# Two transformer blocks on one core: order of the gated units, their low part and one sum within each feed-forward step

## The reference, cut to what matters

```python
ffn = (jax.nn.silu(h2 @ w_gate[l]) * (h2 @ w_up[l])) @ w_down[l]
x = x + gt2 * ffn
...
h = h + (jax.nn.silu(y @ w_gate[i]) * (y @ w_up[i])) @ w_down[i]
```

## Time and profile before

| what | value |
|---|---|
| median of 3 runs | 2380.46 us (2379.41 to 2380.8) |
| the profiled execution, its own time | 2379.61 us |
| span of the profile (first to last instruction) | 2377.9 us |
| TensorE busy | 2244.1 us, 94% |
| VectorE busy | 1938.7 us, 82% |
| ScalarE busy | 1365.9 us, 57% |
| mean granted clock of TensorE | 0.996 |
| steps with gate, up and down together | 20 (10 in each network) |

### The profile page before, as it was taken

The page is one execution under the profiler, slowest core; times in us unless marked ns, Lnnn a source line. Parts: engine busy times, 40 slices in busy tenths (PEclk is TensorE's granted clock), DMA queues, the critical chain, the costliest instruction groups (busy, mean ns, idle before and its releaser), DMA issues.

```text
span 2377.9 us, 30985 instructions
## 1 busy us (share of the span) xinstructions
PE 2244.1 (94%) x10284; PEld 1760.2 (74%) x10284; DVE 1938.7 (82%) x2192; ACT 1365.9 (57%) x1688; POOL 87.9 (4%) x124
## 2 busy tenths in 40 slices
PE   6999999998999999999999999989999999999998
PEld 3577657876777777777778887867777777777786
DVE  4377788989888889988885998688898888888865
ACT  3233475565666666666665444546666666666654
POOL 1101030000000000000010000000000000000020
PEclk9999999999999999999999999999999999999999
DMA  9999986755655565656646555655555565656554
GB/s 392 415 364 371 383 325 239 305 189 167 195 185 188 185 192 179 189 186 187 195 150 214 177 185 169 230 176 186 189 182 186 186 193 187 193 185 191 180 177 151
DMA packets 131567, 518.23 MB, mean 218 GB/s; under 512 B 14497, under 2 KB 20257, under 8 KB 118305
## 3 DMA queue, kind: packets, MB, share of 16 engines
q1 hardware_dynamic: 121552, 449.11, 57.5%
q0 software_dynamic: 9216, 67.11, 6.9%
q10 hardware_dynamic: 720, 0.99, 0.1%
HBM read 512.96 MB, written 4.19 MB: 217 GB/s over the span
## 4 chain that ended last, share of the span: by engine, by line
PE 48%; DVE 20%; issue 9%; ACT 5%; DVEq 1%; DMA 0%; ACTq 0%; SPq 0%
PE ps L2495 28%; PE ps L2673 17%; DVE sum_w_lo L1686 5%; DVE w_lo L1679 3%; ACT w_hi_more L975 3%; DVE sum_raw L1725 2%; DVE sum_raw L1704 2%; DVE w_lo L1969 2%; DVE raw L1710 1%; DVE raw_more L1710 1%; ACT sum_w_hi L864 1%; PE ps L2483 1%; ACT w_hi L975 1%; PE ps L2637 1%; DVE gate L2238 1%
## 5 line engine op out<-in xcount | busy, mean ns | idle before, releaser
L975 ACT ACTIVATE w_hi<-raw 128x1024 fp32r<-128x1024 f32 (+1 forms) x432 | 447.5, 1048 | 352.3 <-PE ps L2673 258.0
L1969 DVE TENSOR_TENSOR w_lo<-raw,w_hi 128x1024 fp32r<-128x1024 f32 (+1 forms) x242 | 292.6, 1218 | 153.1 <-ACT w_hi L975 148.6
L2673 PE MATMUL ps<-w_hi,fm_hi 128*128 128x512 f32 (+1 forms) x840 | 331.4, 394 | 6.9 <-DVE w_lo L1969 5.2
L2673 PE MATMUL ps<-w_lo,fm_hi 128*128 128x512 f32 (+1 forms) x864 | 334.2, 387 | 0.0
L864 ACT ACTIVATE sum_w_hi<-sum_raw 128x1024 fp32r<-128x1024 f32 x180 | 189.6, 1053 | 204.6 <-DVE sum_raw L1704 149.0
L2673 PE MATMUL ps<-w_hi,fm_lo 128*128 128x512 f32 (+1 forms) x776 | 299.6, 386 | 0.0
L1686 DVE TENSOR_TENSOR sum_w_lo<-sum_raw,sum_w_hi 128x1024 fp32r<-128x1024 f32 x180 | 219.5, 1220 | 50.0 <-ACT sum_w_hi L864 47.7
L1679 DVE TENSOR_TENSOR w_lo<-raw,w_hi_more 128x1024 fp32r<-128x1024 f32 x180 | 214.6, 1220 | 16.8 <-ACT w_hi_more L975 13.0
L1679 DVE TENSOR_TENSOR w_lo<-raw,w_hi 128x1024 fp32r<-128x1024 f32 x180 | 218.0, 1220 | 7.5
L975 ACT ACTIVATE w_hi_more<-raw 128x1024 fp32r<-128x1024 f32 x198 | 201.9, 1048 | 35.8 <-DVE raw L1710 29.7
L2673 PEld LDWEIGHTS ps<-w_hi,fm_hi 128*128 128x128 f32 x840 | 157.7, 188 | 63.1 <-issue 23.7
(11 more groups left out here) (399 smaller groups left out, 4631.7 us busy)
## 6 DMA issues: line engine op xcount, KB each, us to landing
raw<-in_w_up SPq DMA_DIRECT2D x152, 512.0 KB, 3.5
raw<-in_w_down SPq DMA_DIRECT2D x132, 512.0 KB, 3.5
ada_raw<-in_w_ada POOLq DMA_DIRECT2D x64, 1024.0 KB, 10.7
raw<-in_w_in SPq DMA_DIRECT2D x120, 512.0 KB, 4.0
raw<-in_w_gate SPq DMA_DIRECT2D x112, 512.0 KB, 4.0
raw<-in_w_out SPq DMA_DIRECT2D x64, 512.0 KB, 3.6
raw_more<-in_w_gate SPq DMA_DIRECT2D x64, 512.0 KB, 3.5
raw_more<-in_w_down SPq DMA_DIRECT2D x44, 512.0 KB, 3.5
```

The lines of the kernel that those rows point to most:

```text
L975: act.activation(hi_tile(like)[:, :, 0:width], raw_tile(like)[:, :, 0:width], ACT.Copy).then_inc(hi_ready, 1)
L1969: dve.tensor_tensor(lo_tile(p)[:, :, 0:width], raw_tile(p)[:, :, 0:width], hi_tile(p)[:, :, 0:width], ALU.subtract).then_inc(lo_dve, 1)
L2673: last = pe.matmul(banks[t][:, 0:width], a, b, start=kt == 0 and k == 0, stop=kt == kts - 1 and k == 2)
```

## The change

Five edits, all of order:

- TensorE transposes the gated units behind the first form `b11`, ahead of `c`.
- VectorE makes `hid_lo` behind the low parts of b21 and of sum w, no longer ahead of sum z.
- ScalarE rounds sum u of the next step ahead of the last `sums_out` of this step, no longer at the head of the step.
- At the head of a feed-forward VectorE does `early(0)` ahead of `hidden_first`, and the three `mixed_rest` stand between low parts; ScalarE rounds two mixtures ahead of one weight block.
- `ungated` is cleared by one memset on GpSimd, and ScalarE waits for it (`cleared`) ahead of its first `early_his`.

```diff
-TURN_AFTER = ("c", 0)
+TURN_AFTER = ("b11", 0)
...
             def gate_up_his(i):
 
-                sum_hi(i, "u", 0)
                 hidden_hi(i + done + 1)
...
+            splits(f + UP + AHEAD + 1, f + UP + AHEAD + 2)
+            mixture_hi(0)
+            mixture_hi(1)
+            splits(f + UP + AHEAD + 2, f + UP + AHEAD + 3)
+            mixture_hi(2)
             splits(f + UP + AHEAD + 3, a)
+            if not done:
+                act.wait_ge(cleared, 1)
             early_his(0, 0)
             early_his(0, 1)
+            sum_hi(0, "u", 0)
             with act.Fori(0, FFN_STEPS - 2) as i:
                 gate_up_his(i)
                 down_his(i)
                 early_his(i + 1, 0)
                 sums_out(i, 2)
                 early_his(i + 1, 1)
+                sum_hi(i + 1, "u", 0)
                 sums_out(i, 3)
...
             mla_operands()
+            pool.wait_ge(emb_spilled, 16)
+            pool.memset(ungated[:, :, :], 0.0).then_inc(cleared, 1)
             pool_block2(pool, rests, rest_loop)
...
                 sum_low(i, "u", 0)
-                hidden_lo(i + done + 1)
                 sum_z(i, 0)
                 piece_low(i, "b21", 0)
                 sum_low(i, "w", 0)
+                hidden_lo(i + done + 1)
                 piece_low(i, "c", 1)
...
             mix_operands(1)
-            rests(f + UP + 2, f + UP + 3)
+            rests(f + UP + 2, f + UP + 4)
+            mixed_rest(0)
+            rests(f + UP + 4, f + UP + 5)
             mix_operands(2)
-            rests(f + UP + 3, f + UP + 4)
-            for k in range(GROUPS):
-                mixed_rest(k)
-            rests(f + UP + 4, f + UP + 6)
-            if not done:
-                dve.wait_ge(emb_spilled, 16)
-            clear(0)
-            rests(f + UP + 6, a)
-            clear(1)
+            rests(f + UP + 5, f + UP + 6)
+            mixed_rest(1)
+            rests(f + UP + 6, f + UP + 7)
+            mixed_rest(2)
+            rests(f + UP + 7, a)
+            early(0)
             hidden_first()
-            early(0)
```

More of the change, by code:

```diff
@@ L489, in build @@
         y_ready, sub_ready, sub_squared = sem("y_ready"), sem("sub_ready"), sem("sub_squared")
-        pool_step = sem("pool_step")
+        pool_step, cleared = sem("pool_step"), sem("cleared")
         x_ready, x_cols, x_squared = sem("x_ready"), sem("x_cols"), sem("x_squared")
@@ L939, in act_ffn, with mixture_hi @@
             act.sem_inc(gate_read, 1)
-            splits(f + UP + AHEAD + 1, f + UP + AHEAD + 3)
-            for k in range(GROUPS):
+            def mixture_hi(k):
                 act.wait_ge(mixed_raw, GROUPS * (1 if done else 0) + k + 1)
                 act.activation(mixed_hi[k][:, :, :, :], mixed_tiles[k][:, :, :, :], ACT.Copy).then_inc(mixed_hi_ready, 1)
+            splits(f + UP + AHEAD + 1, f + UP + AHEAD + 2)
[3 more added lines that the diff above has]
+            mixture_hi(2)
             splits(f + UP + AHEAD + 3, a)
+            if not done:
+                act.wait_ge(cleared, 1)
             early_his(0, 0)
             early_his(0, 1)
+            sum_hi(0, "u", 0)
             with act.Fori(0, FFN_STEPS - 2) as i:
@@ L1843, in rests @@
                     rest(p)
-            def clear(t):
-                if not done:
-                    link(dve.memset(ungated[:, t, :], 0.0))
             rests(f + UP if done else f + AHEAD + 3, f + UP)
```

## The result

The changed kernel takes **2309.97 us** (median of 4 runs, 2306.3 to 2310.75) beside 2380.63 us for the kernel before; the ratio is 0.970, with a 95% interval of 0.968 to 0.972. The profiled execution took 2310.75 us, its span is 2309.0 us. The forecast was 2308, its range 2298 to 2333.

What follows compares the result with a forecast made beforehand. The prediction took VectorE's late run, which TensorE waits for, as the bound. Steps 18 x 3.13 = 56.3 plus heads 16.2 gave 72.5 off 2379.61, so 2307.1, or 2308 us as a median; range 2298 to 2333.

Steps and rivals of the forecast that it cites:

- Period: One feed-forward step, repeating every 67.16 us before: claimed to take 64.03 us, 3.13 less.
- W: Point in each step where TensorE starts the last form w; forecast at 575.9 in the first network.
- T: Point in each step where TensorE's transposes of the gated units start; forecast at 541.95 in the first network.
- slot of 2.44: Rival: the operation moved into VectorE's run costs 2.44 us, pause included, 1.3 more than the rows' spacing; 2332 us; chance 0.02.
- the rival: ScalarE's 1.2 us of room between the `ungated` copy and `hid_hi` closes, eating the turn's gain; 2357 us; chance 0.06.
- So it does the low part of sum u and sum z at once: VectorE at the step's end, after b22's low part at 680.0: both done by about 682.3, cover 2.6 us.
- Late weight block: Rival: sum z asks for b21 some 7 us earlier and its load is late; periods stay, 2364 us; chance 0.04.
- up to 0.3 more per head: Clock loss in each head: 1.65 us lost again after TensorE's wait makes its path 33.9, adding up to 0.3 us.
- Gain 8.6: Head of the first feed-forward: W at 575.9 instead of 584.5, 8.6 us earlier.
- Gain 8.2: Head of the second feed-forward: W at 1611.1 instead of 1619.3, 8.2 us earlier.
- Sum: Whole run: 18 periods give 56.3 us and heads 16.2, together 72.5 off the profiled 2379.61.
- TensorE becomes the bound: Rival: waits in VectorE's run shrink too, so TensorE's own work sets a period of 62.3; 2277 us; chance 0.03.

Runs made afterwards that it cites:

- lo_back: The changed kernel with VectorE's `hid_lo` put back ahead of sum z in each step; 2316.26 us.
- z_run: The changed kernel with sum z of the second group computed a second time into a spare tile, inside VectorE's run from b21's low part to the last form; 2331.46 us.
- head_back: The changed kernel with both heads as before: old order on VectorE and ScalarE, memsets on VectorE, none on GpSimd; steps stay changed; 2321.71 us.
- turn_back: The changed kernel with the transposes of the gated units put back behind the conventional product `c`; 2363.27 us.
- turn_only: The kernel before with only the transposes of the gated units moved behind the first form `b11`; 2328.9 us.
- z_gap: The changed kernel with sum z of the first group computed a second time into a spare tile, where VectorE stands idle ahead of b21's low part; 2307.32 us.
- b21_lo_place: The changed kernel with ScalarE rounding the first group's b21 a step earlier, `hid_lo` directly behind b21's low part, and an own tile for the second group's sum u; 2273.01 us.
- sum_back: The changed kernel with ScalarE's rounding of the first group's sum u put back at the head of each step; 2312.43 us.
- b21_early: The changed kernel with ScalarE's rounding of the first group's b21 moved to the end of the step before, ahead of the copies out; 2297.19 us.

## Why the prediction was right, step by step

- **Period.** Predicted 64.03, measured 64.05. Each of its three terms stands: W to T 30.12 (30.12), T to b21's low part 3.07 (3.08), the run to W 30.84 (640.97 - 610.13 = 30.84).
- **Price of a moved VectorE operation.** 1.14 by the spacing in the rows; lo_back and z_run confirm it. Neither the flush of the Trainium skill (VectorE: DVE Perf Modes, The DRAIN you can't avoid) nor the slot of 2.44 is seen.
- **`hid_lo`.** Predicted at T + 5.35, measured T + 5.36, and TensorE never waits for it in the steps.
- **ScalarE.** The rounding of sum u fell into its idle stretch (603.70), the copy of `ungated` keeps 1.21 us of room ahead of `hid_hi`, as the rival had it. "So it does the low part of sum u and sum z at once" was right; what it is worth by itself (0.25 us a step) I had not worked out.
- **Late weight block.** Not seen: sum z follows at once, at 606.29.
- **Heads.** T in the first network was predicted at 541.95 and came at 542.04; W was predicted at 575.9 and came at 576.90. The term "up to 0.3 more per head" for the clock was too small, and it was placed on TensorE's own path to W, where it was not. T to W took 34.86 instead of 33.92: after 3.26 us of idle the clock fell again, matmuls started 0.43 apart for 3.6 us, a fall as in the earlier trace rows. So TensorE released the tile of the first sum u late, at T + 9.69 instead of T + 8.07, and VectorE stood 0.82 us for it (the row at 551.73 above); the rest of its run was as long as in any step. In the second network the eight transposes themselves took 1.94 us, against 1.04 in a step, so the high part of the gated units came late, b21's low part only at T + 3.99, and W 34.83 behind T:

```profile
1543.22 1.94 PE L2487 MATMUL ps<-ident,hidden 128*128 128x128 f32 x8 [2.31 <-DVE hidden L1639]
```

- **What the heads are made of.** "Gain 8.6" and "Gain 8.2" were 7.6 and 7.4 at the first W, without the shift between the networks. They are sums of all that moved ahead of the first W, and they mix causes: the reordering alone brought 11.7 in all (head_back), and the rest fits the first steps' share of the turn, which turn_back has outside its 18 periods too (1.6 in the first network).
- **GpSimd.** The memset was bounded by 7.0 us and took 3.53, and started at 498.83, 7.2 us after the spill was issued. No wait of ScalarE for GpSimd is listed: costed at nothing, and it cost nothing.

```profile
498.83 3.53 POOL L1355 MEMSET ungated<- 128x4096 f32 x1 [161.78 <-DMA emb_kept<-emb_first]
```

- **Sum.** Between the medians lie 70.7 us. The sum was made for the profiled executions, and these are 68.9 apart (2379.61 and 2310.75) where 72.5 were predicted. Periods 18 x 3.11 = 56.0 (predicted 56.3) and heads about 14.4 (16.2; 15.0 at the first W, of which `last_lo`, where the count ends, shows 0.3 less in each network) make 70.4, and 1.4 us of the first network's gain are not there any more when the second network's mixtures start (35.3 at the end of the first, 33.9 there). These 1.4 us are a fall of the clock that came in some profiles and not in others. Behind the first network TensorE waits 2.62 us for `x`, and in the changed kernel's profile matmuls start 0.43 apart after it:

```profile
1197.46 1.11 PE L2641 MATMUL ps<-ident,x 128*128 128x128 f32 x8 [2.62 <-DVE x L1840]
...
1198.79 0.63 PE L2677 MATMUL ps<-w_hi,last_lo 128*128 128x512 f32 x1
1199.22 0.63 PE L2677 MATMUL ps<-w_lo,last_hi 128*128 128x512 f32 x1
```

  The granted clock was 0.66 over 1199.00 to 1203.00. The same wait passed at 1.00 in the profiles of the kernel before, of turn_only and of z_gap, and z_gap is the changed kernel with one operation more; from `last_lo` to the second network's first mixture these three took 335.8 to 335.9 us, the changed kernel 337.3. That the forecast missed the median by 2.0 us only, where the sum was 3.6 short, is luck of the two profiled executions: one lies 0.85 under the median that the prediction started from, the other 0.8 above its own.
- **Rival "TensorE becomes the bound".** Its period of 62.3 was right as a floor: b21_lo_place reaches 62.17. Its condition was not met by this change: b21_lo_place has three more edits, and between the two bounds lay a third at 63.36, the single tile of sum u, which my list of rivals did not have.

## What to carry to other kernels

When two engines hand work to each other in a loop, mark on both the points where one waits for the other, and write the period as a sum of stretches between these points; an edit is then worth what it does to one of the stretches, for this change to 0.02 us a step, and the same operation costs 0 or 1.11 us by which side of a mark it stands on. Where the sum failed (sum_back by 0.15, b21_early by 0.2 and more), another chain or another wait had become the one that ends last. An idle stretch ahead of an operation is useful only to operations that need nothing of what is being waited for, so those go ahead of the wait (the seven operations of `early(0)` ahead of the gated product, sum z ahead of the low part of the gated units). Once a run starts earlier, look for the buffer that it writes next: a steady step of the old trace does not show such a wait while the engine is late enough, and how late it is (0.69 us here) bounds what the earlier start can bring. A disturbed step, here the first one, can show it already.

## What I had not expected of the hardware

The clock fall behind an idle stretch reaches further than the price in the old trace. After 3.26 us of idle, matmuls started 0.43 us apart for 3.6 us (granted clock 0.56, so mostly at the lower level of 1.2 GHz); after 2.31 us of idle in the second network, the eight transposes took 1.94 instead of 1.04 us, and since these transposes are what ScalarE and VectorE wait for, their whole chain moved by 0.9 us. The fall did not come each time alike: the same turn of the first network took 1.06 us in the changed kernel and 1.91 to 1.94 us in head_back, b21_early and lo_back, with idle times of 3.2 us in the last two. In z_gap it did not come at all: after 3.27 us of idle the transposes took 1.06 us and the granted clock was 1.00 over 541.50 to 546.00.
